# A feed-forward step that multiplies the four 512-column blocks of its two units first, and its four 256-column blocks after them

## The chip, the core and the metric

The kernel runs on one core of a Trainium2 chip. The metric is the device time of one execution in microseconds (us), and lower is better. Engines are named as in the profile: PE is TensorE's matmul stream, PEld its weight loads, DVE is VectorE, ACT is ScalarE, POOL is GpSimd, SP issues most of the DMAs.

## What is computed

Two transformer blocks run one behind the other on 256 tokens of width 1024, all in float32. The change touches the three feed-forward networks (FFNs): the one that ends the first block, and the two around the attention of the second block.

```python
def _rmsnorm(x, g):
    return xf * lax.rsqrt(jnp.mean(xf * xf, axis=-1, keepdims=True) + EPS) * g

def _conv_glu_ffn(h, w_up, conv_w, conv_b, w_down):      # FFN 0, D_FF = 2816
    a, v = jnp.split(h @ w_up, 2, axis=-1)
    ap = jnp.pad(a, ((0, 0), (CONV_W - 1, 0), (0, 0)))
    a = sum(ap[:, j:j + T] * conv_w[j] for j in range(CONV_W)) + conv_b
    return (jax.nn.gelu(a, approximate=False) * v) @ w_down

def swiglu(x, w_gate, w_up, w_down):                      # FFN 1 and FFN 2, D_FF = 2816
    return (jax.nn.silu(x @ w_gate) * (x @ w_up)) @ w_down

x = x + _conv_glu_ffn(_rmsnorm(x, norm_ffn_g), ...)       # end of the first block
x = x + 0.5 * swiglu(rmsnorm(x, ffn1_norm), ...)          # start of the second block
x = x + token_mixer(rmsnorm(x, mix_norm), ...)
x = x + 0.5 * swiglu(rmsnorm(x, ffn2_norm), ...)
```

## The kernel before

**Numbers in two parts.** TensorE multiplies in a reduced float32 format (`F32R`), so each operand is kept as a high part and the rest, the low half. A weight unit is 128 x 2048 values. SP loads it into one of three `raw` buffers, ACT copies it to `wh` (line 977, semaphore `w_hi`), DVE takes the difference to `wl` (line 1419, `w_lo`). There are three `wh`/`wl` slots, and a unit may be copied when TensorE has finished with the unit three places ahead of it in the plan (`unit_end`).

**The activations.** `hT` holds the normalized input turned, 8 blocks k of 128 rows; high parts in its first half, low parts in its second. `hT_both(k)` is a moving operand of 512 columns, high and low part together; `hT_at(k)[0]` is the high part alone, 256 columns.

**A step of an FFN.** Each FFN f has 11 steps j of 256 hidden columns. A step has two units, the gate's ("up", f, j, 0) and the value's ("up", f, j, 1), here called a and v. Each unit is two tiles m of 128 columns. For one tile `crossed` issues eight matmuls of 512 columns (weight high part, line 379) and then eight of 256 (weight low part, line 381) into one PSUM bank. Unit a's tiles lie in banks 0 and 1, unit v's in banks 6 and 7 (`UP = Banks(0, 6)`), in every step. A unit's last matmul signals `ps_full`. Behind the two units of step j come the 24 matmuls of 512 columns of the down-projection of step j-1, four accumulators of six each (`down_part`).

**What is done with the sums.** ACT copies the half of the sums that comes from the low parts to `Am` (`second_sums`, line 1265), DVE adds it to the other half (`up_sums`, line 1504, two instructions); that frees the unit's two banks. For unit a, DVE then multiplies by the tokens' scale (line 1956), in FFN 0 DVE and ACT do the convolution (lines 1288 and 1969) and ACT the Gelu (1293), in the others ACT does the Silu (1299). DVE scales again (1973), adds up unit v (1504), multiplies the two (1979); ACT copies the product to `yTh` (1311) and DVE takes the low half `yTl` (1994), which signals `y_lo`. The down-projection of step j waits for `y_lo` of step j. Between these, each engine makes the weight parts that `begin(...)` names, in the order of the program; nothing is reordered at run time.

**The ends of an FFN.** Step 0 is `up_pair`: since the normalized input of blocks 4 to 7 is there before that of blocks 0 to 3, it goes over k in two halves, with `norm_turn` (eight transposes of X, line 448) in the first half and `spread` (line 462, which spreads the tokens' scale over the partitions, copied out by DVE line 1478) in the second. Between step 0 and step 1 there is no down-projection. Behind step 10 of FFN 0 and 1 come the down-projection of step 9 and directly that of step 10. In FFN 2 the down-projections of steps 8, 9 and 10 are kept to the end, so step 10 follows step 9 directly.

**The seam.** When the accumulators of the last down-projection are full, DVE adds them to X (`x_part`, line 1940), TensorE turns X (`norm_turn`), ACT and DVE make the high parts and low halves of the next `hT` (lines 995 and 1448: `turn_lo_gained`), and the next FFN or the attention begins. The low halves `wl` of the next two units are made in between.

Of the kernel before, what the change touches and what calls it, by code (L numbers as in the profile page):

```python
# [129 lines left out]
def build(nc, plan, I, out):  # L130
    ctx = ExitStack()
    with ctx:
# [141 lines left out]
        def full(key):  # L274
            return ps_full[at[key][0]], at[key][1]

        def free(key):
            return ps_free[at[key][0]], at[key][2]
# [14 lines left out]
        def hT_both(k):  # L293
            return hT[:, :].rearrange("p (s n) -> p s n", s=2)[:, :, k * 256:k * 256 + 256]
# [55 lines left out]
        def pe_program(pe):  # L350
# [9 lines left out]
            def weights(i):  # L360
                pe.wait_ge(w_lo, i + 1)
# [9 lines left out]
                return ins  # L371


            def crossed(o, lw, ks, first, last, ready=None):
                lh, ll = lw
                for k in ks:
                    if ready is not None and (k == ks[0] or k % 2 == 0):
                        pe.wait_ge(*ready(k))
                    pe.matmul(o, lh(k), hT_both(k), start=first and k == ks[0], stop=False)  # L379
                for k in ks:  # L380
                    ins = pe.matmul(o[:, 256:512], ll(k), hT_at(k)[0], start=False, stop=last and k == ks[-1])  # L381
                return ins
# [33 lines left out]
            def take_two(key):  # L416
                b = UP.take()
                return b, [take(key, b), take(key + ("x",), b + 1, False)]

            def up_out(key):  # L420
                i = U[key]
                b, ts = take_two(key)
                weights(i)
                for m in range(2):
                    ins = crossed(ts[m], weight_left(i, 256, m * 128), EIGHT, True, True)
                ins.then_inc(ps_full[b], 1)
                unit_end[i] = full(key)

            def toks_out(key, banks, src=hT_at, ready=None, mid=None):
                i, b = U[key], banks.take()  # L430
# [55 lines left out]
                        if half and j == 0:  # L486
                            spread(k)

            def up_pair(key0, key1, k):
                keys, bs, ts = (key0, key1), [0, 0], [None, None]  # L490
                for half, ks in enumerate(((4, 5, 6, 7), (0, 1, 2, 3))):
                    for j in range(2):
                        i = U[keys[j]]
                        if not half:
                            bs[j], ts[j] = take_two(keys[j])
                            weights(i)
                        for m in range(2):
                            ins = crossed(ts[j][m], weight_left(i, 256, m * 128), ks, half == 0, half == 1,
                                          (lambda k2: free(("n", k, k2 // 2))) if j == 0 and m == 0 else None)
                        if half:  # L500
                            ins.then_inc(ps_full[bs[j]], 1)
                            unit_end[i] = full(keys[j])
                        if not half and j == 0:
                            norm_turn(k, 0)
                            norm_turn(k, 1)
                        if half and j == 0:
                            spread(k)

# [353 lines left out]

            def ffn(f, k, k_next):
                for j in range(11):
                    if j == 0:
                        up_pair(("up", f, 0, 0), ("up", f, 0, 1), k)
                    else:
                        up_out(("up", f, j, 0))
                        up_out(("up", f, j, 1))
                    if 1 <= j < (9 if k_next is None else 10):  # L870
                        down_begin(f, j - 1)
                        for n in range(4):
                            ins = down_part(f, j - 1, n)
                        ins.then_inc(down_done, 1)
                        unit_end[U["down", f, j - 1]] = (down_done, 10 * f + j)
                if k_next is None:
                    last_units(f)
                    return
                down_begin(f, 9)
                for n in (2, 3, 0, 1):  # L880
                    ins = down_part(f, 9, n)
                ins.then_inc(down_done, 1)
                unit_end[U["down", f, 9]] = (down_done, 10 * f + 10)
                down_begin(f, 10)
                for n in (2, 3, 0, 1):
                    down_part(f, 10, n).then_inc(ps_full[acc[n]], 1)
                    if n == 0:
                        T.n = 0
                        norm_turn(k_next, 2)
                        norm_turn(k_next, 3)  # L890
                unit_end[U["down", f, 10]] = full(("acc", f, 1))
# [517 lines left out]
        def dve_program(dve):  # L1409
# [533 lines left out]
            def ffn(f, k, scale, k_next):  # L1943
                for j in range(11):
                    n = 11 * f + j
                    ka, kv = ("up", f, j, 0), ("up", f, j, 1)
                    c, g = P[j % 2], PT[j % 2]
                    gv = g if j else PT[1]
                    if j == 0:
                        norm_pair(ka, k)  # L1950
                    else:
                        begin(ka)
                    up_sums(g[:, :], ka)
                    for m in range(2):
                        dve.wait_ge(*free((ka, ka + ("x",))[m]))
                    dve.tensor_tensor(v3(g), v3(g), by_token(2), ALU.mult).then_inc(up_made, 1)
                    if j == 0:
                        up_sums(gv[:, :], kv)
                        lo_to(U[ka] + 3)
                    else:  # L1960
                        begin(kv)
                    if f == 0:
                        dve.wait_ge(cv_in, 2 * j + 2)
                        for d in (1, 2):
                            if d == 2:
                                dve.wait_ge(*seq.now())
                            for m in range(2):
                                w = c[:, m * 256 + d:m * 256 + 256]
                                dve.scalar_tensor_tensor(out=w, in0=g[:, m * 256:m * 256 + 256 - d],
                                                         scalar=col("cw", 22 * (2 - d) + 2 * j + m), in1=w, op0=ALU.mult,  # L1970
                                                         op1=ALU.add).then_inc(*(seq.next() if d == 1 else (cv_out, 1)))
                    dve.wait_ge(ff_act, n + 1)
                    dve.tensor_tensor(v3(c), v3(c), by_token(2), ALU.mult).then_inc(act_made, 1)
                    if j:
                        up_sums(gv[:, :], kv)
                    dve.wait_ge(act_made, n + 1)
                    for m in range(2):
                        dve.wait_ge(*free((kv, kv + ("x",))[m]))
                    dve.tensor_tensor(g[:, :], gv[:, :], c[:, :], ALU.mult).then_inc(ff_y, 1)
                    late = k_next is None and j >= 9  # L1980
                    if 1 <= j < 10 and not late:
                        begin(("down", f, j - 1))
                    elif j == 0 and f == 0:
                        lo_to(U[ka] + 4)
                    if late and j == 10:
                        lo_to(U["down", f, 10])
                    if f == 0 and 6 <= j < 8:
                        dve.wait_ge(bias_neg, 4)
                        piece = heads(BIGT[:, j * 1024 - 4096:j * 1024 - 3072], 4)
                        dve.tensor_tensor(piece, piece, times.unsqueeze(1).to_broadcast([128, 4, 256]),  # L1990
                                          ALU.subtract).then_inc(bias_made, 1)
                    o = j % 2 * 512
                    dve.wait_ge(y_hi, n + 1)
                    dve.tensor_tensor(yTl[:, o:o + 512], g[:, :], yTh[:, o:o + 512].bitcast(F32),
                                      ALU.subtract).then_inc(y_lo, 1)
                if k_next is None:
                    return
                begin(("down", f, 9))
                x_part(f, 2, scale)
                x_part(f, 3, scale)  # L2000
                lo_half(U["down", f, 10] + 2, 0)
                x_part(f, 0, scale)
                turn_lo_gained(("n", k_next, 2), 2, k_next)
                turn_lo_gained(("n", k_next, 3), 3, k_next)
                x_part(f, 1, scale)
                lo_half(U["down", f, 10] + 2, 1)

            project(1)
            ffn(0, 1, 1.0, 2)
# [362 lines left out]
```

## Time and profile before

| | |
|---|---|
| median of 3 runs | 967.41 us (967.31 to 967.98) |
| the profiled execution's own time | 968.34 us |
| its span, first to last instruction | 966.5 us |
| mean granted TensorE clock over the span | 0.999 |
| HBM traffic | 172 MB read, 1 MB written |
| ACT's longest kind of wait in the FFNs (line 1265, for PE) | 148.2 us in 48 waits |

The page's busy times say how full each engine is. A PE that is busy all the time shows little of what a change of order does; that is read from the timeline (start, length, engine, line, operation, operands, number of merged instructions, and in brackets the idle time before them with its cause). In the timeline a matmul's length includes the time that it takes to drain, so the pace of a stream is read from the distance of starts.

### The profile page before, as it was taken

How to read it: one execution, taken by the hardware profiler on the slowest of the kernel's cores; microseconds unless marked ns; L12 is line 12 of the kernel's file. 1: busy time of each engine (PE TensorE's matmuls, PEld its weight loads, DVE VectorE, ACT ScalarE, POOL GpSimd, SP SyncE). 2: the span in 40 equal slices, each digit the busy share in tenths (PEclk: the TensorE clock that was granted, in tenths of full speed). 3: DMA queues.
4: the chain of work that ended last, by engine and by line, in shares of the span. 5: the costliest groups of instructions: out<-in, count | busy, mean ns of one | idle time of the engine just before them, and what ended most of it. 6: DMA issues, size and time to landing. Idle time of an engine off the chain costs nothing.

```text
span 966.5 us, 15618 instructions
## 1 busy us (share of the span) xinstructions
PE 957.3 (99%) x6446; PEld 862.5 (89%) x6446; DVE 708.5 (73%) x1011; ACT 519.3 (54%) x658; POOL 70.1 (7%) x152
## 2 busy tenths in 40 slices
PE   9999999999999999999999999999999999999997
PEld 8999999999988888888888888889999788888886
DVE  5788767887777877787786667568678678576665
ACT  6674756555446656555664444446545555444544
POOL 1010223343210000000000000000002000000000
PEclk9999999999999999999999999999999999999999
DMA  9744454443464564655456565553433546555541
GB/s 337 299 172 145 162 175 137 170 141 126 170 237 170 209 218 175 217 175 199 150 177 215 177 215 174 193 198 133 175 132 131 180 147 218 195 198 178 192 154 43
DMA packets 26534, 174.17 MB, mean 180 GB/s; under 512 B 3552, under 2 KB 3808, under 8 KB 6368
## 3 DMA queue, kind: packets, MB, share of 16 engines
q1 hardware_dynamic: 25600, 170.11, 50.5%
q10 hardware_dynamic: 864, 3.07, 0.8%
q8 instruction: 51, 0.84, 0.3%
q14 instruction: 19, 0.16, 0.0%
HBM read 172.12 MB, written 1.05 MB: 179 GB/s over the span
## 4 chain that ended last, share of the span: by engine, by line
PE 96%; DVE 2%; ACT 1%; DMA 1%; issue 0%; ACTq 0%; DVEq 0%
PE ps L369 52%; PE ps L379 25%; PE ps L381 13%; PE ps L658 2%; PE ps L448 1%; PE ps L672 1%; PE ps L705 1%; DMA raw<-in_units 1%; PE ps L575 1%; DVE wl L1419 0%; ACT wh L977 0%; PE ps L719 0%; PE ps L686 0%; PE ps L462 0%; DVE X L1940 0%
## 5 line engine op out<-in xcount | busy, mean ns | idle before, releaser
L1419 DVE TENSOR_TENSOR wl<-raw,wh 128x2048 fp32r<-128x2048 f32 (+1 forms) x153 | 348.2, 2277 | 65.9 <-ACT wh L977 65.1
L977 ACT ACTIVATE wh<-raw 128x2048 fp32r<-128x2048 f32 (+1 forms) x156 | 296.3, 1900 | 73.7 <-PE ps L369 67.3
L379 PE MATMUL ps<-hT,wh 128*128 128x512 f32 x1056 | 266.6, 392 | 0.2 <-DVE hT L1448 0.2
L379 PEld LDWEIGHTS ps<-hT,wh 128*128 128x128 f32 x1056 | 190.7, 189 | 35.4 <-issue 0.6
L369 PE MATMUL ps<-hT,wh 128*128 128x256 f32 (+1 forms) x912 | 168.7, 286 | 1.6 <-DVE wl L1419 1.3
L381 PEld LDWEIGHTS ps<-hT,wl 128*128 128x128 f32 x1056 | 145.6, 190 | 11.4
L381 PE MATMUL ps<-hT,wl 128*128 128x256 f32 x1056 | 149.1, 282 | 0.0
L369 PEld LDWEIGHTS ps<-hT,wh 128*128 128x128 f32 (+1 forms) x912 | 141.0, 190 | 3.7 <-DVE wl L1419 1.5
L369 PE MATMUL ps<-wh,hT 128*128 128x256 f32 (+1 forms) x704 | 142.1, 296 | 0.0
L369 PE MATMUL ps<-hT,wl 128*128 128x256 f32 (+1 forms) x456 | 128.9, 283 | 0.0
L1265 ACT ACTIVATE Am<-ps 128x512 f32<-128x512 f32 x66 | 39.2, 594 | 150.9 <-PE ps L381 148.2
L369 PE MATMUL ps<-wh,yTh 128*128 128x512 f32 (+1 forms) x298 | 116.4, 390 | 0.0
L369 PEld LDWEIGHTS ps<-wh,hT 128*128 128x128 f32 x704 | 113.3, 191 | 3.1 <-issue 0.5
L369 PE MATMUL ps<-wl,yTh 128*128 128x512 f32 (+1 forms) x298 | 115.9, 389 | 0.0
L369 PE MATMUL ps<-wh,yTl 128*128 128x512 f32 (+1 forms) x298 | 115.6, 388 | 0.0
L369 PE MATMUL ps<-wl,hT 128*128 128x256 f32 (+1 forms) x352 | 102.9, 292 | 0.0
L1504 DVE TENSOR_TENSOR PT<-ps,Am 128x256 f32<-128x256 f32 x132 | 49.8, 419 | 67.7 <-ACT Am L1265 67.6
L369 PEld LDWEIGHTS ps<-hT,wl 128*128 128x128 f32 (+1 forms) x456 | 86.4, 190 | 0.2
L369 PEld LDWEIGHTS ps<-wl,hT 128*128 128x128 f32 x352 | 67.3, 191 | 1.3
L369 PEld LDWEIGHTS ps<-wh,yTl 128*128 128x128 f32 x298 | 56.0, 188 | 11.8
L369 PEld LDWEIGHTS ps<-wh,yTh 128*128 128x128 f32 x298 | 56.1, 188 | 10.8 <-issue 0.2
L369 PEld LDWEIGHTS ps<-wl,yTh 128*128 128x128 f32 x298 | 56.1, 188 | 10.2
(255 smaller groups left out, 830.2 us busy)
## 6 DMA issues: line engine op xcount, KB each, us to landing
raw<-in_units SPq DMA_DIRECT2D x155, 1024.0 KB, 4.9
BIGT<-in_bias ACTq DMA_DIRECT2D x1, 2048.0 KB, 7.6
XT<-in_x_turned SPq DMA_DIRECT2D x4, 256.0 KB, 5.7
raw<-in_units SPq DMA_DIRECT2D x4, 256.0 KB, 5.9
raw<-in_units SPq DMA_DIRECT2D x2, 512.0 KB, 7.3
X<-in_x SPq DMA_DIRECT2D x1, 1024.0 KB, 9.0
Hn<-in_mem SPq DMA_DIRECT2D x1, 1024.0 KB, 10.6
XT<-in_mem_turned SPq DMA_DIRECT2D x1, 1024.0 KB, 12.6
```

The costliest lines, as they stand in the source:

```text
L369: ins = pe.matmul(o, l(k), r(k), start=first and k == ks[0] and j == 0, stop=last and k == ks[-1] and j == 2)
L379: pe.matmul(o, lh(k), hT_both(k), start=first and k == ks[0], stop=False)
L381: ins = pe.matmul(o[:, 256:512], ll(k), hT_at(k)[0], start=False, stop=last and k == ks[-1])
L448: ins = pe.transpose(t[:, q * 128:q * 128 + 128], src[:, m * n + k * 128:m * n + k * 128 + 128], ident)
L575: ins = pe.matmul(t[x:x + w, q * w + w - z:q * w + w], s[:, x:x + w], s[:, x + a:x + a + z], start=True, stop=True)
L658: ins = pe.matmul(t[:, x:z], l, r, start=True, stop=True)
L672: ins = pe.transpose(t[:, j * 128:j * 128 + 128], src[:, o:o + 128], ident)
L705: ins = pe.matmul(o[64 * j:64 * j + 64, 128 * kb:256], v[:, x:x + 64], turned(a, i + j)[:, c], start=kb == 0, stop=kb == 1)
L977: act.activation(wh[j % NS][:, 0:n], raw[j % NR][:, 0:n], ACT.Copy).then_inc(w_hi, 1)
L1265: act.activation(v3(crossed_out(n)), t, ACT.Copy).then_inc(cross_made, 1)
L1419: dve.tensor_tensor(wl[j % NS][:, 0:n], raw[j % NR][:, 0:n], wh[j % NS][:, 0:n].bitcast(F32), ALU.subtract).then_inc(w_lo, 1)
L1504: dve.tensor_tensor(d[:, m, :], t[:, m, :], v3(crossed_out(n))[:, m, :], ALU.add).then_inc(*emptied((key, key + ("x",))[m]))
```

## The change

`crossed` is split into `wide` (the 512-column matmuls) and `narrow` (the 256-column ones). `up_both` replaces two calls of `up_out`: it issues the 32 wide matmuls of units a and v, then the 16 narrow ones of a, then the 16 of v. A wide part waits for `w_hi` of its unit only; `w_lo` is waited for ahead of the narrow part. `up_pair` does the same in each of its two halves over k. At the seam DVE's order of work is another.

```diff
-            def crossed(o, lw, ks, first, last, ready=None):
-                lh, ll = lw
+            def wide(o, lh, ks, first, ready=None):
                 for k in ks:
                     if ready is not None and (k == ks[0] or k % 2 == 0):
                         pe.wait_ge(*ready(k))
                     pe.matmul(o, lh(k), hT_both(k), start=first and k == ks[0], stop=False)
+
+            def narrow(o, ll, ks, last):
                 for k in ks:
                     ins = pe.matmul(o[:, 256:512], ll(k), hT_at(k)[0], start=False, stop=last and k == ks[-1])
                 return ins
...
-            def up_out(key):
-                i = U[key]
-                b, ts = take_two(key)
-                weights(i)
-                for m in range(2):
-                    ins = crossed(ts[m], weight_left(i, 256, m * 128), EIGHT, True, True)
-                ins.then_inc(ps_full[b], 1)
-                unit_end[i] = full(key)
+            def up_both(*keys):
+                bs, ts = [0, 0], [None, None]
+                for j in range(2):
+                    bs[j], ts[j] = take_two(keys[j])
+                    pe.wait_ge(w_hi, U[keys[j]] + 1)
+                    for m in range(2):
+                        wide(ts[j][m], weight_left(U[keys[j]], 256, m * 128)[0], EIGHT, True)
+                for j in range(2):
+                    weights(U[keys[j]])
+                    for m in range(2):
+                        ins = narrow(ts[j][m], weight_left(U[keys[j]], 256, m * 128)[1], EIGHT, True)
+                    ins.then_inc(ps_full[bs[j]], 1)
+                    unit_end[U[keys[j]]] = full(keys[j])
...
                         for m in range(2):
-                            ins = crossed(ts[j][m], weight_left(i, 256, m * 128), ks, half == 0, half == 1,
-                                          (lambda k2: free(("n", k, k2 // 2))) if j == 0 and m == 0 else None)
-                        if half:
-                            ins.then_inc(ps_full[bs[j]], 1)
-                            unit_end[i] = full(keys[j])
+                            wide(ts[j][m], weight_left(U[keys[j]], 256, m * 128)[0], ks, half == 0,
+                                 (lambda k2: free(("n", k, k2 // 2))) if j == 0 and m == 0 else None)
                         if not half and j == 0:
                             norm_turn(k, 0)
                             norm_turn(k, 1)
+                    for j in range(2):
+                        weights(U[keys[j]])
+                        for m in range(2):
+                            ins = narrow(ts[j][m], weight_left(U[keys[j]], 256, m * 128)[1], ks, half == 1)
+                        if half:
+                            ins.then_inc(ps_full[bs[j]], 1)
+                            unit_end[U[keys[j]]] = full(keys[j])
                         if half and j == 0:
                             spread(k)
...
-                begin(("down", f, 9))
                 x_part(f, 2, scale)
                 x_part(f, 3, scale)
-                lo_half(U["down", f, 10] + 2, 0)
-                x_part(f, 0, scale)
+                begin(("down", f, 9))
                 turn_lo_gained(("n", k_next, 2), 2, k_next)
                 turn_lo_gained(("n", k_next, 3), 3, k_next)
+                x_part(f, 0, scale)
                 x_part(f, 1, scale)
-                lo_half(U["down", f, 10] + 2, 1)
+                lo_to(U["down", f, 10] + 2)
```

On TensorE, in a step from 1 to 10 before the change: one tile after the other, wide and narrow in turns. `ps` are the PSUM banks; the first row is unit a, the fifth is unit v.

```order
L379 MATMUL ps<-hT,wh 128x512 [waits w_lo,ps_free1,ps_free0]
L379 MATMUL ps<-hT,wh 128x512 x7
L381 MATMUL ps<-hT,wl 128x256 x8
L379 MATMUL ps<-hT,wh 128x512 x8
L381 MATMUL ps<-hT,wl 128x256 x8
L379 MATMUL ps<-hT,wh 128x512 [waits w_lo,ps_free7,ps_free6]
L379 MATMUL ps<-hT,wh 128x512 x7
L381 MATMUL ps<-hT,wl 128x256 x8
L379 MATMUL ps<-hT,wh 128x512 x8
L381 MATMUL ps<-hT,wl 128x256 x8
L369 MATMUL ps<-wh,yTh 128x512 [waits y_lo,w_lo]
```

The same step on TensorE after the change; the third and the seventh row begin unit v, and the last row is the down-projection behind the step.

```order
L378 MATMUL ps<-hT,wh 128x512 [waits w_hi,ps_free1,ps_free0]
L378 MATMUL ps<-hT,wh 128x512 x15
L378 MATMUL ps<-hT,wh 128x512 [waits w_hi,ps_free7,ps_free6]
L378 MATMUL ps<-hT,wh 128x512 x15
L382 MATMUL ps<-hT,wl 128x256 [waits w_lo]
L382 MATMUL ps<-hT,wl 128x256 x15
L382 MATMUL ps<-hT,wl 128x256 [waits w_lo]
L382 MATMUL ps<-hT,wl 128x256 x15
L369 MATMUL ps<-wh,yTh 128x512 [waits y_lo,w_lo]
```

Unit a's last narrow matmul stood after 32 of the step's 64 matmuls and now stands after 48; unit v's first wide one stood after 32 and now after 16.

On DVE, at the seam between FFN 0 and FFN 1 before the change. `wl1` belongs to the next FFN's unit a, `wl2` to its unit v; `X<-ps,X` are the four `x_part` (accumulators 2, 3, 0, 1), `hT` the low halves of the turned X.

```order
L1994 TENSOR_TENSOR yTl<-PT0,yTh 128x512 [waits y_hi]
L1419 TENSOR_TENSOR wl1<-raw1,wh1 128x2048 [waits w_hi]
L1940 SCALAR_TENSOR_TENSOR X<-ps,X 128x512 [waits ps_full2]
L1940 SCALAR_TENSOR_TENSOR X<-ps,X 128x512 [waits ps_full3]
L1428 TENSOR_TENSOR wl2<-raw2,wh2 128x1024 [waits w_hi]
L1940 SCALAR_TENSOR_TENSOR X<-ps,X 128x512 [waits ps_full4]
L1448 SCALAR_TENSOR_TENSOR hT<-ps,GT,hT 128x256 [waits turn_hi]
L1448 SCALAR_TENSOR_TENSOR hT<-ps,GT,hT 128x256
L1448 SCALAR_TENSOR_TENSOR hT<-ps,GT,hT 128x256 [waits turn_hi]
L1448 SCALAR_TENSOR_TENSOR hT<-ps,GT,hT 128x256
L1940 SCALAR_TENSOR_TENSOR X<-ps,X 128x512 [waits ps_full5]
L1428 TENSOR_TENSOR wl2<-raw2,wh2 128x1024
```

The same place on DVE after the change.

```order
L2003 TENSOR_TENSOR yTl<-PT0,yTh 128x512 [waits y_hi]
L1949 SCALAR_TENSOR_TENSOR X<-ps,X 128x512 [waits ps_full2]
L1949 SCALAR_TENSOR_TENSOR X<-ps,X 128x512 [waits ps_full3]
L1428 TENSOR_TENSOR wl1<-raw1,wh1 128x2048 [waits w_hi]
L1457 SCALAR_TENSOR_TENSOR hT<-ps,GT,hT 128x256 [waits turn_hi]
L1457 SCALAR_TENSOR_TENSOR hT<-ps,GT,hT 128x256
L1457 SCALAR_TENSOR_TENSOR hT<-ps,GT,hT 128x256 [waits turn_hi]
L1457 SCALAR_TENSOR_TENSOR hT<-ps,GT,hT 128x256
L1949 SCALAR_TENSOR_TENSOR X<-ps,X 128x512 [waits ps_full4]
L1949 SCALAR_TENSOR_TENSOR X<-ps,X 128x512 [waits ps_full5]
L1428 TENSOR_TENSOR wl2<-raw2,wh2 128x2048 [waits w_hi]
```

The first two `x_part` went ahead of `wl1`, the first half of `wl2` went from the middle to the end, and the third `x_part` behind the low halves of the turned X.

## Rows read from the trace of the kernel before

**Rows 1.** The page, busy time of each engine over the span

```profile
PE 957.3 (99%) x6446; PEld 862.5 (89%) x6446; DVE 708.5 (73%) x1011; ACT 519.3 (54%) x658; POOL 70.1 (7%) x152
```

**Rows 2.** Timeline, PE, two tiles of FFN 1's step 2 behind a down-projection

```profile
504.96 1.98 PE L379 MATMUL ps<-hT,wh 128*128 128x512 f32 x8
...
506.77 1.11 PE L381 MATMUL ps<-hT,wl 128*128 128x256 f32 x8
...
507.72 2.00 PE L379 MATMUL ps<-hT,wh 128*128 128x512 f32 x8
...
509.56 1.12 PE L381 MATMUL ps<-hT,wl 128*128 128x256 f32 x8
```

**Rows 3.** Timeline, PE, FFN 0's step 10, then down-projections 9 and 10

```profile
457.26 2.00 PE L379 MATMUL ps<-hT,wh 128*128 128x512 f32 x8
...
462.85 0.40 PE L369 MATMUL ps<-wh,yTh 128*128 128x512 f32 x1
...
468.32 0.47 PE L369 MATMUL ps<-wh,yTh 128*128 128x512 f32 x1
```

**Rows 4.** Timeline, ACT and DVE, first and last part of step 10's chain in FFN 0

```profile
457.46 0.60 ACT L1265 ACTIVATE Am<-ps 128x512 f32<-128x512 f32 x1 [3.64 <-PE ps L381]
...
467.48 0.69 DVE L1994 TENSOR_TENSOR yTl<-PT,yTh 128x512 fp32r<-128x512 f32 x1 [0.70 <-ACT yTh L1311]
```

**Rows 5.** Timeline, ACT and DVE, step 10's chain in FFN 1

```profile
643.62 0.60 ACT L1265 ACTIVATE Am<-ps 128x512 f32<-128x512 f32 x1 [3.64 <-PE ps L381]
...
648.27 0.69 DVE L1973 TENSOR_TENSOR P<-P,RB 128x512 f32<-128x512 f32 x1
...
650.73 0.69 DVE L1979 TENSOR_TENSOR PT<-PT,P 128x512 f32<-128x512 f32 x1
652.12 0.69 DVE L1994 TENSOR_TENSOR yTl<-PT,yTh 128x512 fp32r<-128x512 f32 x1 [0.70 <-ACT yTh L1311]
```

**Rows 6.** Timeline, PE, ACT and DVE, end of FFN 2's step 0 and start of step 1

```profile
785.33 0.61 PE L462 MATMUL ps<-diag,ones 128*128 128x128 f32 x4
...
788.58 2.00 PE L379 MATMUL ps<-hT,wh 128*128 128x512 f32 x8
...
785.53 0.60 ACT L1265 ACTIVATE Am<-ps 128x512 f32<-128x512 f32 x1 [2.61 <-PE ps L381]
...
786.75 0.42 DVE L1478 COPY RB<-ps 128x256 f32<-128x256 f32 x1
787.20 0.76 DVE L1504 TENSOR_TENSOR PT<-ps,Am 128x256 f32<-128x256 f32 x2
```

**Rows 7.** Timeline, PE, FFN 2, end of step 9 and start of step 10

```profile
931.70 1.11 PE L381 MATMUL ps<-hT,wl 128*128 128x256 f32 x8
932.65 2.00 PE L379 MATMUL ps<-hT,wh 128*128 128x512 f32 x8
```

**Rows 8.** Timeline, PE and DVE, seam between FFN 0 and FFN 1

```profile
472.82 1.09 PE L448 MATMUL ps<-C,X 128*128 128x128 f32 x8
...
475.47 1.43 PE L379 MATMUL ps<-hT,wh 128*128 128x512 f32 x4 [0.16 <-DVE hT L1448]
...
471.49 1.28 DVE L1940 SCALAR_TENSOR_TENSOR X<-ps,X 128x512 f32<-128x512 f32 x2
...
474.45 1.66 DVE L1448 SCALAR_TENSOR_TENSOR hT<-ps,GT,hT 128x256 fp32r<-128x256 f32 x4
```

**Rows 9.** Timeline, ACT, FFN 0's step 4, first part of the sums and v's next weights

```profile
357.78 0.60 ACT L1265 ACTIVATE Am<-ps 128x512 f32<-128x512 f32 x1 [3.64 <-PE ps L381]
...
366.21 1.91 ACT L977 ACTIVATE wh<-raw 128x2048 fp32r<-128x2048 f32 x1
```

**Rows 10.** Windows of the start and the end: us, busy (instructions), then PEclk, DMA share, GB/s

```profile
2.00:4.00 2.00, 2.00 (x11) 2.00 (x11) 0.00 (x0) 1.14 (x2) 1.09 (x3) 1.00 0.86 261
...
960.00:961.00 1.00, 0.41 (x4) 0.20 (x2) 0.78 (x3) 0.61 (x3) 0.00 (x0) 1.00 0.82 305
...
964.00:965.00 1.00, 0.00 (x0) 0.00 (x0) 0.00 (x0) 0.00 (x0) 0.00 (x0) 0.70 0.80 307
```

More of the change, by code:

```diff
@@ L487, in norm_pair, with up_pair @@
                             spread(k)
-            def up_pair(key0, key1, k):
-                keys, bs, ts = (key0, key1), [0, 0], [None, None]
+            def up_pair(keys, k):
+                bs, ts = [0, 0], [None, None]
                 for half, ks in enumerate(((4, 5, 6, 7), (0, 1, 2, 3))):
                     for j in range(2):
-                        i = U[keys[j]]
                         if not half:
                             bs[j], ts[j] = take_two(keys[j])
-                            weights(i)
+                            pe.wait_ge(w_hi, U[keys[j]] + 1)
                         for m in range(2):
-                            ins = crossed(ts[j][m], weight_left(i, 256, m * 128), ks, half == 0, half == 1,
-                                          (lambda k2: free(("n", k, k2 // 2))) if j == 0 and m == 0 else None)
-                        if half:
-                            ins.then_inc(ps_full[bs[j]], 1)
-                            unit_end[i] = full(keys[j])
+                            wide(ts[j][m], weight_left(U[keys[j]], 256, m * 128)[0], ks, half == 0,
+                                 (lambda k2: free(("n", k, k2 // 2))) if j == 0 and m == 0 else None)
                         if not half and j == 0:
@@ L864, in ffn @@
                 for j in range(11):
+                    keys = ("up", f, j, 0), ("up", f, j, 1)
                     if j == 0:
-                        up_pair(("up", f, 0, 0), ("up", f, 0, 1), k)
+                        up_pair(keys, k)
                     else:
-                        up_out(("up", f, j, 0))
-                        up_out(("up", f, j, 1))
+                        up_both(*keys)
                     if 1 <= j < (9 if k_next is None else 10):
```

## The prediction

> **What bounds the kernel now.** I read the page's busy times first: PE is busy for 99% of the span, DVE for 73%, ACT for 54% [rows 1]. So the time is the length of TensorE's stream, plus whatever holes a change tears into it. The change adds and removes no matmul. It can therefore do two things only: alter the pace inside the stream, or alter when TensorE waits. I read both from the timeline.
>
> The pace is read from distances of starts. Eight wide matmuls behind other wide ones take 1.81 us (504.96 to 506.77), eight narrow ones 0.95, and eight wide ones behind narrow ones 1.84 (507.72 to 509.56) [rows 2]. A step thus costs 1.81 + 3 x 1.84 + 4 x 0.95 = 11.13 us, and the down-projection behind it 5.47 (462.85 to 468.32) [rows 3].
>
> Waits depend on one chain. When unit a's last narrow matmul has gone, ACT starts on its sums 0.20 us later (457.26 to 457.46) [rows 3, 4]; from there ACT and DVE go back and forth until `yTl` is made. In FFN 0 that takes 10.71 us, 457.46 to 468.17 [rows 4]. TensorE's next matmul, the first of down-projection 10, stands at 468.32 and is 0.08 us longer than its like [rows 3]: the chain ends just when it is wanted. I take 0.23 us from DVE's end to the stream running again, from this place. There is no slack at all at this point before the change, and that is where it is decided.
>
> **The change part by part.** I count from the start of a step's first wide matmul.
>
> *New times in a step.* 32 wide take 4 x 1.81 = 7.25 us, unit a's 16 narrow ones 1.91: its sums are complete at 9.16, and ACT starts on them at 9.36. Before, that was at 1.81 + 1.84 + 2 x 0.95 + 0.20 = 5.75. Everything that hangs on unit a comes 3.6 us later. Unit v's sums are complete at 11.08, the step ends there, and the down-projection at 16.55.
>
> *Pace.* Three of four changes from narrow to wide go, 0.03 us each [rows 2], less the 0.01 by which a narrow run of eight is shorter than eight full gaps: 0.06 a step. With 30 steps 1 to 10 and three steps 0, which I give the same: **-2.0 us**. Bounds: 0, and -3.0 (33 x 0.09). The Trainium skill, in "TensorE: Matmul & The Clock Gate", section "Back-to-back issue gap", gives a matmul's gap from its columns alone, so a change of length would cost nothing; by it this term would be 0 and the time 2 us longer. This trace does not agree with it in the 0.03 us.
>
> *Ordinary steps, 1 to 9.* The next step's unit a wants banks 0 and 1 at 16.55, unit v wants banks 6 and 7 and its high weights at 16.55 + 3.63 = 20.18. The tightest place is FFN 0 in the steps in which ACT also turns the sign of a piece of the bias table: there v's next high weights are ready 10.34 us after ACT began on a's sums (357.78 to 368.12) [rows 9], now at 19.70. The work that hides this is 0.48 us, of which 0.23 is latency. I count 0; were it gone in those four steps, it would cost some tenths each. `yTl` ends at most 13.3 us after the chain's start, at 22.7, and is wanted at 27.6.
>
> *Down-projection 10 of FFN 0.* It stands directly behind down-projection 9, so it is wanted at 16.55. The chain ends at 9.36 + 10.71 = 20.07, and the stream goes on at 20.30. That is a hole of 3.75 us where 0.08 was: **+3.67 us**. Queued behind the waiting matmul is all of TensorE's work. Unit v does not matter here: its sums are complete at 11.08, well before DVE comes to them.
>
> *The same in FFN 1.* Without the convolution, DVE's second scaling ends 5.34 us after ACT's start (643.62 to 648.96); then come unit v's sums, 0.76 [rows 6], the product, 0.69, with 0.05 between, and from the product's end (651.42) to that of `yTl` (652.81) 1.39 us [rows 5]: 8.23. So 17.59, with latency 17.82, against 16.55: **+1.27 us**. Before, this chain was done in time.
>
> *FFN 2, step 9 to step 10.* Step 10 follows directly [rows 7]. Its unit a wants banks 0 and 1 at 11.08; they come free 1.39 us after 9.36, at 10.75: no wait, by 0.1. Its unit v wants banks 6 and 7 at 11.08 + 3.63 = 14.71; DVE frees them after the second scaling and the two additions, at 9.36 + 5.34 + 0.68 = 15.38, with latency 15.6: **+0.9 us**. Down-projection 10 of FFN 2 has 12 matmuls of down-projection 9 and all of 8 ahead of it; by the same sums it comes out a tenth of a us ahead. I count 0, with 0.3 as upper bound.
>
> *Step 0 to step 1, three times.* No down-projection lies between. Unit a's sums are now complete just ahead of `spread`, and behind it stand only v's narrow ones: TensorE wants banks 0 and 1 at 0.44 (four transposing matmuls of 0.11) + 0.95 = 1.39 us after `spread` starts. DVE must first copy `spread`'s result, ready 0.62 after its start (785.33, 0.61 long), the sums follow 0.45 later (786.75 to 787.20) and take 0.76 [rows 6]: 0.62 + 0.45 + 0.76 + 0.23 = 2.06. **+0.67 us each, +2.0**. Before, 788.58 lay 0.6 behind the end of these additions. Bounds: 0, if TensorE's arrival slips for another reason, and 1.0 each, if DVE comes late from making `wl`.
>
> *Seams.* Between FFN 0 and FFN 1 the stream of down-projection 10 ran from 468.40; its third quarter ended at 468.40 + 4.08 = 472.48, but the turning of X began at 472.82, since DVE's two `x_part` began only at 471.49 [rows 8], behind `wl`. Now they go first: accumulator 3 is full 2.9 us into the stream, `x_part` ends at 3.6, `wl` (2.29) at 5.85, the low halves run from 5.8 to 7.45. Before they ran from 474.45, 6.05 in, to 7.7. TensorE's next FFN, at 475.47 before, starts 0.3 us earlier: **-0.3 us**. Between FFN 1 and the attention `wl` of the second unit is now made whole, behind both other `x_part`: 7.4 + 1.25 + 2.25 = 10.9, with latency 11.1. TensorE arrives there at 6.8 + 24 x 0.12 + 0.87 = 10.55. With 0.1 for the low halves of X, which ACT set before and `wl` sets now: **+0.6 us**; bounds 0 and 1.0. In the FFNs `wl` of unit v is wanted only behind all wide matmuls, so there its delay is covered.
>
> **The sum.** -2.0 + 3.67 + 1.27 + 0.9 + 2.0 - 0.3 + 0.6 = +6.1 us. The profiled execution took 968.34 us, 0.93 above the median of 967.41, and would take 974.4; against the median the forecast is **973.5 us**.
>
> **The rivals.** *The clock falls in the hole.* After TensorE's last matmul, which ends in the window 960 to 961, the granted clock falls within 964 to 965, from 2.4 to 1.2 GHz [rows 10]: some 4 us of idle time. The hole in FFN 0 leaves TensorE idle for about 3.5. At the start of the kernel 128-column matmuls stand 0.18 to 0.2 us apart [rows 10] against the 0.11 of `spread`, for over 4 us; a fall would cost about half of such a stretch, 2 us: 975.5. Against it: the hole is shorter than the idle time at the end. 12 in 100. The Trainium skill's "TensorE: Matmul & The Clock Gate", section "What's actually happening", has the clock go down on idleness.
>
> *The bank waits stay hidden.* If TensorE's stream and DVE's additions fit between step 0 and 1 and between steps 9 and 10, 2.9 us go and 970.6 us is left. For it: these are the sums with the smallest margins. Against it: nothing in DVE's order can go ahead of the copy. 10 in 100.
>
> *Faster.* Were the chain from unit a's sums to `yTl` covered at step 10, only the pace and the seam would be left: -2.0 - 0.3 + 0.6 and a bank wait or two, about 966 us; with none, 965.7. This is decided where the chain of FFN 0 would be shorter than 16.55 - 9.36 - 0.23 = 6.96 us. It is 10.71, without any wait for unit v in it. 3 in 100. Between this and the forecast, no change that can be measured: 3 in 100.
>
> **How the numbers follow.** The forecast has 72 in 100. Its own range, from the bounds of the small terms, is 972 to 975. The range for 8 in 10 takes in most of the two slower rivals: 971.0 to 975.8. A change under 0.2% (1.9 us) can't be told from none here. Faster 0.03, same 0.03, slower 0.94.
>
> **What would show it.** In the profile after: a wait of TensorE of 3.5 to 3.8 us ahead of down-projection 10 in FFN 0, released by DVE's `yTl`; one of about 1.3 in FFN 1; about 0.9 ahead of unit v's wide matmuls of step 10 in FFN 2; three of about 0.7 between steps 0 and 1; the 32 wide matmuls of a step in 7.25 us, the 32 narrow in 3.83. The turning of X between FFN 0 and 1 waits no longer. Wrong would be the forecast if the narrow run of 32 keeps another pace than 0.12 (0.01 each is 10 us in all), or if an ordinary step gets a wait of its own: 0.1 us there is 3 us in all.

## The result and the profile after

| | before | after |
|---|---|---|
| median | 967.36 us (967.13 to 967.98, 4 runs) | 975.03 us (973.41 to 975.97, 4 runs) |
| ratio | | 1.0076, 95% interval 1.0065 to 1.0088 |
| profiled execution, its own time | 968.34 us | 974.98 us |
| span | 966.5 us | 973.2 us |
| mean granted TensorE clock | 0.999 | 0.997 |

The change makes the kernel 7.7 us slower. That is inside the range of 971.0 to 975.8 us, 1.5 us above the forecast of 973.5, and at the very end of the forecast's own range of 972 to 975. The runs of after also spread over 2.6 us, against 0.9 before.

The page, busy times of after, to be read beside [rows 1]:

```profile
PE 958.4 (98%) x6446; PEld 864.0 (89%) x6446; DVE 704.7 (72%) x1009; ACT 516.4 (53%) x658; POOL 70.1 (7%) x152
```

PE is busy 1.1 us longer in a span that is 6.7 us longer: most of the loss is idle time. The timeline of PE in after shows an ordinary step (FFN 1, step 2; the row ahead of it is a down-projection's last matmul):

```profile
509.29 0.39 PE L369 MATMUL ps<-wh,yTl 128*128 128x512 f32 x1
509.52 7.42 PE L378 MATMUL ps<-hT,wh 128*128 128x512 f32 x32
516.77 3.40 PE L382 MATMUL ps<-hT,wl 128*128 128x256 f32 x27
```

The 32 wide matmuls take 7.25 us (509.52 to 516.77), as forecast, and no hole lies in them. The window ends at 520, so the last row holds 27 of the 32 narrow ones. From the step's first to its last matmul start, plus 0.12 for the last matmul itself, a step is 11.086 us long, against 11.146 before (two of its tiles stand in [rows 2]). That is 0.060 us, the same to 0.001 us in every step from 2 to 9.

The place that decides, FFN 0's step 10 and the down-projections behind it, in the timeline of after, PE, ACT and DVE; it answers to [rows 3, 4]:

```profile
467.24 0.39 PE L369 MATMUL ps<-wh,yTl 128*128 128x512 f32 x1
471.11 0.47 PE L369 MATMUL ps<-wh,yTh 128*128 128x512 f32 x1 [3.49 <-DVE yTl L2003]
...
472.58 0.63 PE L369 MATMUL ps<-wh,yTh 128*128 128x512 f32 x1
473.01 0.63 PE L369 MATMUL ps<-wl,yTh 128*128 128x512 f32 x1
...
460.28 0.60 ACT L1274 ACTIVATE Am<-ps 128x512 f32<-128x512 f32 x1 [4.77 <-PE ps L382]
...
470.28 0.69 DVE L2003 TENSOR_TENSOR yTl<-PT,yTh 128x512 fp32r<-128x512 f32 x1 [0.69 <-ACT yTh L1320]
```

The chain begins at 460.28 and ends at 470.97: 10.69 us, against 10.71 before. It did not become longer, it began later. TensorE, which is done with down-projection 9 at 467.46, stands still until 471.11. Then comes something that the mean granted clock, 0.997, hides: from the seventh matmul on, starts are 0.43 us apart in place of 0.227. The windows view of after, columns us, busy of PE, PEld, DVE, ACT, POOL (with counts), PEclk, DMA share, GB/s:

```profile
470.00:472.00 2.00, 0.89 (x4) 0.79 (x5) 0.69 (x1) 2.00 (x3) 0.00 (x0) 1.00 0.01 4
472.00:474.00 2.00, 2.00 (x8) 1.58 (x7) 0.69 (x1) 2.00 (x3) 0.00 (x0) 0.63 0.00 0
474.00:476.00 2.00, 2.00 (x7) 1.56 (x6) 0.61 (x2) 0.46 (x2) 0.00 (x0) 0.52 0.00 0
476.00:478.00 2.00, 2.00 (x15) 1.75 (x14) 2.00 (x2) 1.15 (x4) 0.00 (x0) 1.00 0.00 0
```

The granted clock is down at half, 1.2 GHz, for most of 472 to 476, behind 3.5 us in which TensorE was idle and six matmuls at the full pace.

The smaller waits, in the timeline of after: down-projection 10 in FFN 1, unit v of step 10 in FFN 2, and the start of step 1 in FFN 2 with the copy and the sums that it waits for, to be read beside [rows 5, 6, 7]:

```profile
659.66 0.47 PE L369 MATMUL ps<-wh,yTh 128*128 128x512 f32 x1 [1.00 <-DVE yTl L2003]
...
942.86 3.91 PE L378 MATMUL ps<-hT,wh 128*128 128x512 f32 x16 [0.56 <-DVE PT L1513]
...
792.90 0.61 PE L468 MATMUL ps<-diag,ones 128*128 128x128 f32 x4
793.26 1.20 PE L382 MATMUL ps<-hT,wl 128*128 128x256 f32 x8
794.86 1.39 PE L378 MATMUL ps<-hT,wh 128*128 128x512 f32 x5 [0.40 <-DVE PT L1513]
...
793.55 0.42 DVE L1487 COPY RB<-ps 128x256 f32<-128x256 f32 x1 [1.85 <-PE ps L468]
794.00 0.76 DVE L1513 TENSOR_TENSOR PT<-ps,Am 128x256 f32<-128x256 f32 x2
```

The bracket counts idle time from the drained end of the matmul before; measured by the distance of starts the three waits are 1.17, 0.72 and 0.56 us. The last is there in each FFN. The first start-to-start gap behind a wait is 0.08 us longer than the others (about 0.31 in place of 0.227); this comes on top. No ordinary step has a wait, and the down-projections of FFN 2 have none either. Behind FFN 1's hole, with 1.00 us of idle time, the granted clock stays at 1.00.

Where the time went, by how much later than before each landmark of TensorE's stream comes (distance of starts in both traces, from the start of FFN 0, where the profiled execution of after was 0.87 us earlier; nothing ahead of that point was changed):

| stretch | us |
|---|---|
| 30 steps 1 to 10, without the wait in FFN 2's | -1.6 |
| step 0, three times | -0.1 |
| step 0 to step 1, three times | +1.7 |
| FFN 0, end of step 10 to FFN 1: hole 3.6, clock 1.6, seam -0.3 | +4.85 |
| FFN 1, end of step 10 to FFN 2: hole 1.2, seam to the attention 0.5 | +1.8 |
| FFN 2, wait in step 10, and the end | +0.8 |
| sum | +7.5 |

### The profile page after: what moved, and what is told of

Same layout as the page of the kernel before. It is cut to its first block, busy times and chain, and to the rows that moved or that the text cites. A ratio compares the mean times of both kernels' runs of the same rounds, so it can differ in the third digit from the quotient of the medians.

```text
span 973.2 us, 15616 instructions
## 1 busy us (share of the span) xinstructions
PE 958.4 (98%) x6446; PEld 864.0 (89%) x6446; DVE 704.7 (72%) x1009; ACT 516.4 (53%) x658; POOL 70.1 (7%) x152
## 4 chain that ended last, share of the span: by engine, by line
PE 95%; DVE 3%; ACT 1%; issue 0%; DMA 0%; ACTq 0%; DVEq 0%
PE ps L369 51%; PE ps L378 24%; PE ps L382 12%; PE ps L667 2%; DVE wl L1428 1%; PE ps L454 1%; PE ps L681 1%; PE ps L714 1%; ACT wh L986 1%; PE ps L584 1%; DMA raw<-in_units 0%; PE ps L728 0%; PE ps L695 0%; DVE hT L1457 0%; PE ps L468 0%
## 5 line engine op out<-in xcount | busy, mean ns | idle before, releaser
L1428 DVE TENSOR_TENSOR wl<-raw,wh 128x2048 fp32r<-128x2048 f32 (+1 forms) x155 | 352.5, 2276 | 26.6 <-ACT wh L986 25.7
L378 PE MATMUL ps<-hT,wh 128*128 128x512 f32 x1056 | 247.1, 390 | 1.9 <-DVE PT L1513 1.8
L378 PEld LDWEIGHTS ps<-hT,wh 128*128 128x128 f32 x1056 | 197.3, 188 | 44.1 <-DVE PT L1513 2.7
L382 PEld LDWEIGHTS ps<-hT,wl 128*128 128x128 f32 x1056 | 131.6, 192 | 2.8
L382 PE MATMUL ps<-hT,wl 128*128 128x256 f32 x1056 | 133.0, 283 | 0.0
```

Source lines behind the costliest of these rows:

```text
L1428: dve.tensor_tensor(wl[j % NS][:, 0:n], raw[j % NR][:, 0:n], wh[j % NS][:, 0:n].bitcast(F32), ALU.subtract).then_inc(w_lo, 1)
```

## The experiments

**e1_unit: fewer changes of length, without later sums.** This run is the kernel before with steps 1 to 10 changed: each unit goes wide 16, narrow 16. Step 0 and the seam are as before the change.

```diff
+            def up_unit(key):
+                b, ts = take_two(key)
+                weights(U[key])
+                for m in range(2):
+                    wide(ts[m], weight_left(U[key], 256, m * 128)[0], EIGHT, True)
+                for m in range(2):
+                    ins = narrow(ts[m], weight_left(U[key], 256, m * 128)[1], EIGHT, True)
+                ins.then_inc(ps_full[b], 1)
...
                     else:
-                        up_out(("up", f, j, 0))
-                        up_out(("up", f, j, 1))
+                        up_unit(keys[0])
+                        up_unit(keys[1])
```

> Steps 1 to 10 in the order wide 16, narrow 16, unit by unit, step 0 and the seam as before the change. Theory (each change from narrow to wide costs TensorE 0.028 us, each start of a narrow run gives back 0.007): two of three such changes go, so 0.041 us a step, 30 steps, 1.2 us faster than before, about 966.2 us, a step 11.10 us long, and no wait anywhere, since unit a's sums are as early as before. Rival (the changed kernel's 0.060 us a step come from waiting for the high weights instead of the low ones ahead of the wide matmuls): no gain here, 967.4 us, a step 11.145 us long, since this order waits for the low weights as before.

Measured: 966.28 us (965.68 to 966.74), ratio to before 0.9987 (0.9979 to 0.9996). Timeline of e1_unit, PE, the same step as above:

```profile
503.59 3.79 PE L388 MATMUL ps<-hT,wh 128*128 128x512 f32 x16
507.21 2.08 PE L392 MATMUL ps<-hT,wl 128*128 128x256 f32 x16
509.13 3.82 PE L388 MATMUL ps<-hT,wh 128*128 128x512 f32 x16
512.78 2.08 PE L392 MATMUL ps<-hT,wl 128*128 128x256 f32 x16
```

The first wide run takes 3.62 us, the second, behind narrow ones, 3.65; a step is 11.106 us long, 0.040 less than before. The rival is out: this order waits for the low weights ahead of the wide matmuls and gains all the same. What costs time is a narrow run followed by a wide one.

**e2_step10: only the place of the holes undone.** In the changed kernel step 10 of FFN 0 and 1 goes tile by tile as before.

```diff
+                    elif f < 2 and j == 10:
+                        up_out(keys[0])
+                        up_out(keys[1])
                     else:
                         up_both(*keys)
```

> The changed kernel, but step 10 of FFN 0 and FFN 1 goes unit by unit and tile by tile as before the change. Theory (the hole ahead of down-projection 10 comes from unit a's sums being 3.6 us late in that one step, and the slow matmuls behind it from that hole): 3.6 us of waiting and 1.6 us at the lower clock in FFN 0 and 1.2 us of waiting in FFN 1 go, 6.3 us less than the changed kernel, about 968.7 us, and the runs lie within 0.5 us of each other. Rival (DVE is late from the steps before, since its work now comes in one bunch): the hole stays at 2 to 3.7 us, 972 to 975 us.

Measured: 969.04 us (968.70 to 969.33), 6.0 us less than the changed kernel. The holes of 3.65 and 1.17 us and the slow matmuls are gone. But ahead of down-projection 10 of FFN 0 a wait of 0.50 us stays (by the distance of starts), where before had none. Its cause is in the timeline of e2_step10, ACT and DVE:

```profile
456.23 0.60 ACT L1286 ACTIVATE Am<-ps 128x512 f32<-128x512 f32 x1 [1.16 <-PE ps L382]
...
455.51 2.28 DVE L1440 TENSOR_TENSOR wl<-raw,wh 128x2048 fp32r<-128x2048 f32 x1
457.71 0.75 DVE L1525 TENSOR_TENSOR PT<-ps,Am 128x256 f32<-128x256 f32 x2
```

ACT is done with unit a's sums at 456.83, but DVE is still at work on what step 9 left in its late bunch and comes at 457.71. So the rival holds for a seventh, 0.5 us of 3.65: the main part is the step's own order, a small part the order of the step ahead.

**e3_fill: TensorE kept at work in the hole.** Twelve calls of a matmul of ones (24 in the trace) go into a free bank, and nothing uses the result.

```diff
+                if f == 0:
+                    pe.wait_ge(*free(("up", 0, 10, 0)))
+                    for _ in range(12):
+                        pe.matmul(bank[0][:, 0:128], ones[:, :], ones[:, :], start=True, stop=True)
                 down_begin(f, 10)
```

> The changed kernel with 12 matmuls of ones, without use, put into TensorE's hole ahead of FFN 0's down-projection 10, some 2.6 us of work inside 3.65 us of waiting. Theory (the clock fell because TensorE was idle): the hole's end stays where it is, the down-projection behind it runs at 0.227 us a matmul at once, 1.6 us less, about 973.4 us, and the runs are closer to each other than the changed kernel's 973.4 to 976.0. Rival (the slow matmuls are a cost of the late operand yTl, or of something else in that stretch, and not of idle time): 975.0 us, the first eight matmuls 0.427 us apart as before.

Measured: 973.32 us (973.03 to 973.52). Timeline of PE and one window of e3_fill:

```profile
467.07 2.84 PE L896 MATMUL ps<-ones 128*128 128x128 f32 x24
470.73 0.47 PE L369 MATMUL ps<-wh,yTh 128*128 128x512 f32 x1 [0.81 <-DVE yTl L2007]
...
472.00:474.00 2.00, 2.00 (x11) 1.65 (x10) 0.96 (x2) 2.00 (x3) 0.00 (x0) 1.00 0.00 0
```

The down-projection begins no earlier, for it still waits for `yTl`, but the clock stays at 1.00, the kernel is 1.7 us faster than the changed one, and its four runs lie within 0.5 us. The rival is out: the operand is as late as before, and the first matmuls behind the wait keep 0.227 us. Work that computes nothing makes the kernel faster than no work. The Trainium skill ("TensorE: Matmul & The Clock Gate", section "What's actually happening") says that the clock is gated by how busy the engine has been; these traces agree, with a fall behind 3.5 us of idle time and no fall when 2.7 us of it were filled.

**e6_mixed: the new order where the sums may be late.** The kernel before with the new order in steps 1 to 9 (in FFN 2, 1 to 8) and the other steps behind step 0 unit by unit; step 0 and the seam are as before.

```diff
+                    elif j == 10 or (f, j) == (2, 9):
+                        up_unit(keys[0])
+                        up_unit(keys[1])
                     else:
-                        up_out(("up", f, j, 0))
-                        up_out(("up", f, j, 1))
+                        up_both(*keys)
```

> The new order only where the sums may be late: steps 1 to 9 of FFN 0 and 1 and steps 1 to 8 of FFN 2; step 10 of each FFN and step 9 of FFN 2 unit by unit (wide 16, narrow 16); step 0 and the seam as before the change. Theory (five places with waits cost all that was lost, the order itself gives 0.060 us a step): 26 steps at 0.060 and 4 at 0.041, 1.7 us faster than before, 965.7 us, no wait of TensorE that before did not have. Rival (between step 0 and 1 the wait comes from the new order of step 1, not of step 0): three waits of 0.56 us stay and the gain is gone, 967.4 us.

Measured: 966.26 us (965.92 to 966.77), ratio 0.9989 (0.9980 to 0.9998). Steps 1 to 9 take 0.060 us less, the unit-wise ones 0.040, and no wait is left between steps 0 and 1, nor between steps 9 and 10 of FFN 2. But ahead of down-projection 10 of FFN 0 the 0.5 us of e2 are back (0.54): that is the half microsecond by which it misses its forecast, and it makes it no better than e1.

**e8_pair_old: step 0 in the old order, all else as in the changed kernel.** The functions `crossed` and `up_pair` of before, put back.

```diff
-                        up_pair(keys, k)
+                        up_pair(*keys, k)
```

> The changed kernel with step 0 in its order before the change. Theory (the 0.56 us waits between step 0 and 1 come from unit a's sums and the copy of spread's result standing right ahead of step 1): all three are gone, and at the seam between FFN 0 and 1 a wait for v's low weights of 0.4 to 0.5 us comes. Rival (they come from the new order of step 1, which asks for unit v's banks earlier): they stay or move to step 1's unit v.

Measured, in a single run: 973.35 us. Timeline of e8_pair_old, PE, FFN 1:

```profile
490.53 1.08 PE L379 MATMUL ps<-hT,wh 128*128 128x512 f32 x4
491.45 0.64 PE L381 MATMUL ps<-hT,wl 128*128 128x256 f32 x4
491.92 1.32 PE L388 MATMUL ps<-hT,wh 128*128 128x512 f32 x5
```

Step 1's wide matmuls follow at once, in all three FFNs: the 0.56 us waits belong to step 0's order. Three of them make 1.7 us, and by as much this single run is below the changed kernel's median. At the seam, unit v's wide matmuls of step 0 came about 0.25 us later than in before's order of DVE, less than the 0.4 to 0.5 expected.

**e4_seam_old: the old order on DVE at the seam, all else as in the changed kernel.** The last part of the diff is undone.

```diff
+                begin(("down", f, 9))
                 x_part(f, 2, scale)
                 x_part(f, 3, scale)
-                begin(("down", f, 9))
+                lo_half(U["down", f, 10] + 2, 0)
+                x_part(f, 0, scale)
                 turn_lo_gained(("n", k_next, 2), 2, k_next)
                 turn_lo_gained(("n", k_next, 3), 3, k_next)
-                x_part(f, 0, scale)
                 x_part(f, 1, scale)
-                lo_to(U["down", f, 10] + 2)
+                lo_half(U["down", f, 10] + 2, 1)
```

> The changed kernel with DVE's order at the seam as before the change. Theory (the seam has nothing to do with the holes): the 3.65 us hole ahead of down-projection 10 stays as it is and the clock falls again for a stretch that may have another length; X's turning waits 0.3 us again in FFN 0; from FFN 1 to the attention the wait of 0.34 us ahead of the second unit goes. Rival (the holes come from DVE's new order at the seam, since x_part now stands ahead of the low weights): the holes go, 969 us.

Measured, in a single run: 975.83 us. The hole is there to the hundredth (3.65 us), the one in FFN 1 too (1.17): the seam has no part in them. The lower clock lasts longer here than in the changed kernel's trace. Timeline of PE and windows of e4_seam_old:

```profile
470.84 0.77 PE L369 MATMUL ps<-wh,yTh 128*128 128x512 f32 x1 [3.49 <-DVE yTl L2003]
...
470.00:472.00 2.00, 1.16 (x3) 1.01 (x4) 0.89 (x2) 2.00 (x2) 0.00 (x0) 0.52 0.02 4
...
476.00:478.00 2.00, 2.00 (x9) 1.50 (x9) 1.66 (x2) 0.72 (x2) 0.00 (x0) 0.77 0.99 418
```

Here and in e8_pair_old the clock is already at half when TensorE goes on (0.52 and 0.55 over 470 to 472), while in the changed kernel's trace it fell 1.4 us after that. Against e3_fill, 14 matmuls run slow here and 2.9 us are lost; in the changed kernel it is 8 and 1.6 us, in e8_pair_old 7 and 1.5. So the same hole costs another amount in each of the three traces. That the spread of the changed kernel's runs comes from this is not shown trace by trace, but their mean granted clocks go with it: 0.998 in the run of 973.41 us, 0.997 in those of 974.98 and 975.08, 0.995 in the one of 975.97. Between FFN 1 and the attention the wait for the second unit's low weights is gone. What did not come is the expected 0.3 us ahead of X's turning in FFN 0: the turning stands 0.23 us behind the matmul before it (477.65 to 477.88). At the slow pace DVE waits 1.64 us for the second accumulator's sums and is no longer the one that is late. So the -0.3 us of the seam in the table is shown as the work of DVE's new order by e5 alone, at the full clock.

**e5_seam_only: the new seam in the kernel before.** The kernel before with the lines of the diff's last part in their new order.

> The kernel before with the new order on DVE at the seam alone. Theory: between FFN 0 and 1 the turning of X begins 0.3 us earlier, but unit v's low weights now come last and the old step 0 waits for them ahead of v's wide matmuls, 0.4 to 0.5 us; between FFN 1 and the attention 0.1 for the low halves of X and 0.4 to 0.5 for the second unit's low weights: together 0.5 to 0.8 us slower than before, 967.9 to 968.2 us. Rival (the new seam is better by itself at both places): 0.3 to 0.6 us faster, 966.9 us.

Measured: 967.70 us (967.52 to 968.20) against 967.35 beside it, ratio 1.0004 (0.9995 to 1.0013). The time alone decides nothing; the trace does. Between FFN 0 and 1 the turning of X no longer waits, 0.32 us gained, and unit v's wide matmuls come 0.25 us late: -0.06 in all. From FFN 1 to the attention 0.50 us is lost. Together +0.44, just under the lower end of what was expected: `wl` of unit v was 0.2 us less late than worked out.

**e7_best: a version from what was found.** The new order in steps 1 to 8 (FFN 1: to 9), unit by unit in the last two (FFN 1: the last), the new seam between FFN 0 and 1 only, step 0 wide first in its first half over k and unit by unit in its second.

```diff
                         if half:
+                            for m in range(2):
+                                ins = narrow(ts[j][m], weight_left(U[keys[j]], 256, m * 128)[1], ks, True)
...
+                    elif j == 10 or j == 9 and f != 1:
+                        up_unit(keys[0])
+                        up_unit(keys[1])
                     else:
                         up_both(*keys)
```

> The new order in steps 1 to 8 of FFN 0 and 2 and 1 to 9 of FFN 1; steps 9 and 10 (in FFN 1 step 10) unit by unit (wide 16, narrow 16); step 0 in the new order in its first half over k and unit by unit in its second; the new order at the seam between FFN 0 and 1 alone. Theory (DVE works off the bunch of a step in the new order within one step, so one step unit by unit ahead of step 10 takes the 0.5 us wait away that e2 and e6 kept; unit a's sums of step 0 are early again, so banks 0 and 1 are free in time): 25 steps at 0.060, 5 at 0.041, 0.3 at the seam, together 2.0 us less than before, 965.4 us, less than e1. Rival (the backlog on DVE lasts longer than one step): a wait of 0.5 us stays ahead of down-projection 10, 966 us or more.

Measured: 965.35 us (965.15 to 966.58) against 967.35, ratio 0.9981 (0.9972 to 0.9990). Timeline of e7_best, DVE and PE, ahead of down-projection 10 of FFN 0:

```profile
456.50 0.76 DVE L1529 TENSOR_TENSOR PT<-ps,Am 128x256 f32<-128x256 f32 x2 [1.93 <-ACT Am L1290]
...
465.88 0.69 DVE L2019 TENSOR_TENSOR yTl<-PT,yTh 128x512 fp32r<-128x512 f32 x1 [0.70 <-ACT yTh L1336]
...
466.72 0.47 PE L369 MATMUL ps<-wh,yTh 128*128 128x512 f32 x1
```

DVE has 1.93 us to spare again when unit a's sums come, the chain ends at 466.57 and TensorE goes on at 466.72. One step unit by unit is enough to work the bunch off. This version beats both kernels, by 2.0 us the one before.

## Why the prediction was right, point by point

*That the change is slower, by waits and not by pace: right.* e2 shows it by itself: with step 10 of FFN 0 and 1 undone, 6.0 of the 7.7 us are gone. But 1.6 of these 6.0 are the lower clock, which the forecast left out of its sum.

*Pace, forecast -2.0 us.* The ordinary steps gave 0.060 us each, as forecast; steps 1, which follow a wait, gave none, since the longer first gap behind the wait takes it back; steps 0 gave 0.034 on average. Together -1.6 to -1.7 us.

*FFN 0's hole, forecast +3.67.* 3.65 us from start to start, where before has none; the longer first gap behind it stands in both kernels. The step of the working that carries it, "Everything that hangs on unit a comes 3.6 us later", stands: the chain is 10.69 us long, against 10.71.

*FFN 1's hole, forecast +1.27; FFN 2's unit v, +0.9; steps 0 to 1, +0.67 each.* From start to start 1.17, 0.72 and 0.56. The forecast's 0.23 us "from DVE's end to the stream running again" takes in the longer first gap behind a wait, which these three places did not have before; with it they are 1.25, 0.80 and 0.63 (for the last, this 0.07 is the same that steps 1 lose above). So FFN 1 is met within 0.02 us. The two waits for banks are 0.1 and 0.04 smaller, in part because the 0.23 was too large there: in FFN 2 the additions end at 794.76 and TensorE starts at 794.86, 0.10 us later, where behind `yTl` in FFN 0 it is 0.14. *Ordinary steps and FFN 2's down-projection 10, forecast 0.* No wait came there.

*Seams, forecast -0.3 and +0.6.* e5 gives -0.3 at the first and +0.5 at the second. In e5 the gain at the first was given back in part, since the old step 0 wants unit v's low weights early; in the changed kernel their delay is covered by the wide matmuls, as argued: its step 0 of FFN 1 has no such wait.

*What was left out of the sum: the clock.* The prediction had it as the rival "The clock falls in the hole", at 2 us and 12 in 100. It fell in each of the three traces that have the unfilled hole, and e3 shows the cause and the price, 1.7 us by the medians. The forecast with the 1.6 us of the trace is 975.1, and the measured 975.03 is that. The rival came true, then, and not the case that had 72 in 100; the time is inside the range because the range had been drawn to take this rival in. That 2 us was near the price is in part luck. It was taken from the slow matmuls at the kernel's start, where the rows give a granted clock of 1.00 [rows 10], so that they do not show a clock at half; and the price itself went from 1.5 to 2.9 us in three traces. The argument against it, "the hole is shorter than the idle time at the end" (3.5 against 4 us), was no argument: one length of idle time behind which the clock fell gives no bound from below for those behind which it does not. The sum of the other terms, by the traces +5.9 us, was forecast as +6.1: the pace gave some 0.35 us less, and the waits and seams cost some 0.6 less.

*Left open.* The hole ahead of down-projection 10 was not tried at other lengths, so these runs do not say how short it would have to be for the clock to stay: it fell behind 3.5 us of idle time and stayed behind the 1.00 us in FFN 1.

## What to carry to other kernels

Regrouping matmuls on a full TensorE moves the moment at which each result is complete, even if the stream is as long as before: take the time of the last matmul of each consumer's input before and after, and follow it to the next place where the stream has no other work to put in between. In the middle of a pipeline a shift of 3.6 us cost nothing; at its end, where one chain had no slack, it cost all of itself. Treat the last steps of a loop apart from the rest, and leave one step for the engine behind to work off its bunch. And count a hole of some microseconds (3.5 us of idle time here) dearer than its length, because the matmuls behind it may run at half clock.

## What was not expected of the hardware

Filling a hole with useless matmuls paid: 24 of 128 columns, 2.7 us of work, brought 1.7 us. And the price of one and the same hole, 3.65 us in after and e4_seam_old and 3.66 in e8_pair_old, differed from run to run with the stretch at the lower clock: 7, 8 and 14 slow matmuls, nearly all 0.427 us apart, in three traces. The clock fell now before TensorE went on, now 1.4 us after it.

A wide run behind a narrow one costs 0.028 us in its first five matmuls (233, 236, 228, 232 and 231 ns from start to start in before, then 227), and a narrow run's first gap is 113 ns, the others 120. Long runs keep 227 and 120 ns. A wait for a semaphore that has long been reached costs nothing visible: unit v's first wide matmul in a step of after waits for `w_hi` and two banks and stands 227 ns behind the one before it, and its first narrow one, which waits for `w_lo`, 120.
